# A two-layer decoder trunk on one core: a second half of the input projection resident through a layer, in the room of two of fourteen gather slots

## The reference

```python
def layer(x, ...):
    proj = rmsnorm(x, norm1) @ w_in               # 1024 x 2568: q, k, v, output gate, pooling input, gates
    hm = mlstm_mixer(q, k, v, ...)                # 4 heads of 128, chunks, running-max state
    zp = pool_mixer(u_pool, ...)                  # trailing windows 2, 4, 8, 16
    x = x + concat(hm, zp) @ w_out                # 1024 x 1024
    x = x + peer_ffn(rmsnorm(x, norm2), ...)
    x = x + sigmoid(x @ w_gate) * (p @ w_ple)

def peer_ffn(xn, wq, sub_keys, u_tab, v_tab):
    q = xn @ wq                                   # 1024 x 2048, 8 heads
    # per token and head the best 16 of 128 x 128 product keys
    ue = u_tab[eidx]                              # tokens x 8 heads x 16 experts x 1024
    act = gelu(einsum('td,thkd->thk', xn, ue))
    ve = v_tab[eidx]
    return einsum('thk,thkd->td', gate * act, ve)
```

## Time and profile before

| | |
|---|---|
| runs before | 1910.49 us (1908.98 to 1910.65) |
| the profiled execution, its own time | 1893.48 us |
| its span, first to last instruction | 1891.7 us |
| busy: PE / PE weight load / DVE / ACT / POOL | 1079.0 / 499.7 / 978.1 / 192.3 / 998.2 us |
| mean granted TensorE clock | 0.752 |
| DMA | 685.11 MB, mean 362 GB/s over the span |

### The profile page before, as it was taken

One profiled execution on the slowest core, in us unless ns is written; L12 is line 12 of the kernel. 1 busy time (PEld: TensorE's weight loads), 2 busy tenths in 40 slices (PEclk: granted clock), 3 DMA queues, 4 the chain that ended last, 5 costly groups with the idle time before them and its releaser, 6 DMA issues. The chain is left out here.

```text
span 1891.7 us, 17959 instructions
## 1 busy us (share of the span) xinstructions
PE 1079.0 (57%) x6318; PEld 499.7 (26%) x6318; DVE 978.1 (52%) x2585; ACT 192.3 (10%) x332; POOL 998.2 (53%) x1062
## 2 busy tenths in 40 slices
PE   8840257788955835385655874048885522045556
PEld 4420133433412422241112432024341211031113
DVE  1498975523445788954004576951344497850001
ACT  3200021201101200000000212000110000000002
POOL 0156534345465555656666353755446566656663
PEclk9965668789987967697676886578896765576678
DMA  8699869889999999989999799979999999999995
GB/s 333 244 359 379 337 244 410 337 359 399 357 360 406 423 410 421 404 343 419 371 366 386 256 421 365 408 286 418 368 337 366 402 374 381 396 330 372 368 367 206
DMA packets 172759, 685.11 MB, mean 362 GB/s; under 512 B 19616, under 2 KB 21344, under 8 KB 158190
## 3 DMA queue, kind: packets, MB, share of 16 engines
q0 software_dynamic: 152064, 553.72, 75.9%
q1 hardware_dynamic: 20606, 130.25, 17.3%
HBM read 677.66 MB, written 6.59 MB: 362 GB/s over the span
## 5 line engine op out<-in xcount | busy, mean ns | idle before, releaser
L2105 DVE SCALAR_TENSOR_TENSOR rows<-rows,acc 128x1024 f32<-128x1024 f32 x512 | 594.2, 1217 | 49.6 <-issue 26.7
L908 PE MATMUL bank<-wring,turned 128*128 128x512 f32 (+1 forms) x808 | 394.0, 635 | 40.6 <-DMA wring<-in_w 24.3
L1235 PE MATMUL acc<-rows,wz 128*32 128x512 f32 x1952 | 323.1, 783 | 143.6 <-DMA rows<-in_v,index_tb 102.6
L1450 POOL DMA_INDIRECT rows<-in_u,index_A x256 | 240.3, 939 | 303.2 <-DVE rows L2105 123.8
L1450 POOL DMA_INDIRECT rows<-in_v,index_ta x256 | 242.5, 947 | 234.1 <-PE acc L1235 142.2
L1450 POOL DMA_INDIRECT rows<-in_u,index_B x256 | 240.7, 940 | 179.1 <-DVE rows L2105 110.7
L1450 POOL DMA_INDIRECT rows<-in_v,index_tb x256 | 241.1, 942 | 138.7 <-issue 68.1
L908 PEld LDWEIGHTS bank<-wring,turned 128*128 128x128 f32 x808 | 160.5, 207 | 236.7 <-issue 205.7
L1235 PEld LDWEIGHTS acc<-rows,wz 128*32 128x32 f32 x1952 | 69.6, 130 | 351.9 <-issue 347.0
L1185 PE MATMUL bank<-xn_s,consts 128*128 128x128 f32 x256 | 48.6, 334 | 154.3 <-issue 154.3
L1185 PEld LDWEIGHTS bank<-xn_s,consts 128*128 128x128 f32 x256 | 42.9, 243 | 159.9 <-issue 159.9
(11 more groups left out here) (320 smaller groups left out, 1054.4 us busy)
## 6 DMA issues: line engine op xcount, KB each, us to landing
wring<-in_w SPq DMA_DIRECT2D x103, 1024.0 KB
out_sample<-scratch SPq DMA_DIRECT2D x2, 2128.5 KB
scratch<-in_c_s SPq DMA_DIRECT2D x2, 2064.0 KB
rows<-in_u,index_A POOLq DMA_INDIRECT x256
rows<-in_v,index_ta POOLq DMA_INDIRECT x256
rows<-in_u,index_B POOLq DMA_INDIRECT x256
rows<-in_v,index_tb POOLq DMA_INDIRECT x256
kept<-in_w SPq DMA_DIRECT2D x2, 1024.0 KB
```

The lines of the kernel that those rows point to most:

```text
L908: ins = pe.matmul(ps[:, part], turned["A"][:, 4 * h + c, :], w[:, c, part], start=first, stop=end, skip_group_check=True)
L1235: ins = pe.matmul(acc[i * QUAD:(i + 1) * QUAD, c, :], wz[:, i, at:at + QUAD], row, start=first, stop=end, skip_group_check=True)
L1450: pool.indirect_dma_start(out=rows[:, n % RING, :], out_offset=None, in_=a[table], in_offset=bass.IndirectOffsetOnAxis(ap=which[:, at:at + ...
L2105: dve.scalar_tensor_tensor(u, u, 1.0, acc[:, :, :], ALU.mult, ALU.mult, accum_out=dots[kind][:, s:s + 1]).then_inc(u_used, 1)
```

## The change

`RING` becomes 12, and `kept` holds two halves: those of `project` with row half 0 of column blocks 0 and 1. Each has its own pair of semaphores. SP loads both at the start, and each for layer 1 behind its last use in pass 1. The second half so leaves the ring of three: the list of ring halves goes from 104 to 100, four loads of 1 MB less, and the loads into `kept` go from two to four. 8 KB per partition move from `rows` (two slots of 4 KB) to `kept` (one half of 8 KB). The line numbers behind the first hunk are 1 higher than before, behind the last one 2.

```diff
--- before.py
+++ after.py
@@ -40,11 +40,12 @@
 NEG = -1e30
 REMOVED = -3e38
 
-RING = 14
+RING = 12
 GROUP = 4
 DOTS = 2
 QUAD = 32
 TURN = QUAD // 2
+KEPT = 2
 LANE = 32
 HALF = 2 * P
 LATE = (LANE - DEC) // GROUP
@@ -92,7 +93,7 @@
 
 
 def is_kept(e):
-    return e[0] == "project" and e[2:4] == (0, 0)
+    return e[0] == "project" and e[2] < KEPT and e[3] == 0
 
 
 def half_key(e):
@@ -677,7 +678,7 @@
         sb("to_boundary", P, 96)
         wring = sb("wring", P, WRING, 4, BLOCK)
         rows = sb("rows", P, RING, D)
-        kept = sb("kept", P, 4, BLOCK)
+        kept = sb("kept", P, KEPT, 4, BLOCK)
         keys = sb("keys", P, 2 * PH, NKEYS)
         gain2 = sb("gain2", P, D + HALF)
         x = {"A": sb("x_a", P, D), "B": sb("x_b", P, D), "S": sb("x_s", P, HALF)}
@@ -789,7 +790,7 @@
 
         bank_full = [sem(f"bank_full{i}") for i in range(BANKS)]
         bank_free = [sem(f"bank_free{i}") for i in range(BANKS)]
-        kept_in, kept_used = sem("kept_in"), sem("kept_used")
+        kept_in, kept_used = [sem("kept_in_%d" % j) for j in range(KEPT)], [sem("kept_used_%d" % j) for j in range(KEPT)]
         half_used, u_used, v_used = sem("half_used"), sem("u_used"), sem("v_used")
         wz_clear, xn_ready, squared = sem("wz_clear"), sem("xn_ready"), sem("squared")
         xn_scaled, xn_shown = sem("xn_scaled"), sem("xn_shown")
@@ -862,8 +863,8 @@
             def half(e):
 
                 if is_kept(e):
-                    pe.wait_ge(kept_in, 16 * (layer_of(PASS_TILES[e[1]][0]) + 1))
-                    return kept
+                    pe.wait_ge(kept_in[e[2]], 16 * (layer_of(PASS_TILES[e[1]][0]) + 1))
+                    return kept[:, e[2]]
                 n = HALF_OF[e]
                 if e == APART:
                     pe.wait_ge(last_half_in, 16)
@@ -911,7 +912,7 @@
                     closed(ins, name, t, j)
                 elif is_kept((name, p, j, h)):
                     if t == PASS_TILES[p][-1]:
-                        ins.then_inc(kept_used, 1)
+                        ins.then_inc(kept_used[j], 1)
                 elif t == PASS_TILES[p][-1] and (name, p, j) != ("query", 0, 0):
                     ins.then_inc(half_used, 1)
 
@@ -1336,10 +1337,11 @@
                 sp.dma_start(wring[:, n % WRING].rearrange("p c n -> p (c n)"),
                              a["w"][layer, half_index(e)]).then_inc(half_in[n % WRING], 16)
 
-            def load_kept(layer):
-                sp.dma_start(kept[:, :, :].rearrange("p c n -> p (c n)"), a["w"][layer, IN0]).then_inc(kept_in, 16)
-
-            load_kept(0)
+            def load_kept(layer, j):
+                sp.dma_start(kept[:, j].rearrange("p c n -> p (c n)"), a["w"][layer, IN0 + 2 * j]).then_inc(kept_in[j], 16)
+
+            for j in range(KEPT):
+                load_kept(0, j)
             for e in HALVES_IN_ORDER[0:WRING]:
                 load_half(e)
                 if e == HALVES_IN_ORDER[1]:
@@ -1356,8 +1358,8 @@
                     loaded += 1
                 if is_kept(e) and e[4] == PASS_TILES[1][-1]:
 
-                    sp.wait_ge(kept_used, 2)
-                    load_kept(1)
+                    sp.wait_ge(kept_used[e[2]], 2)
+                    load_kept(1, e[2])
                 if e[0] == "layer":
                     layer = e[1]
                     if layer:
```

## The result

The changed kernel takes 1935.53 us (median of four runs, 1925.05 to 1941.89), the kernel before 1909.74 us beside it. The ratio is 1.0132, 95% interval 1.0081 to 1.0182: slower by some 25 us, four times the forecast and outside the range. Measured twice more it is 1.0143 (1.0097 to 1.0189) and 1.0074 (1.0048 to 1.0101).

What follows compares the result with a forecast made beforehand. The 16 DMA engines were taken as the nearest thing to one bound, with gather, POOL and DVE rates nearly equal. Terms of both signs summed to +6.2 us on 1910.5, said as 1916.5 us; the 8-in-10 range was 1900 to 1932.

Steps and rivals of the forecast that it cites:

- Start: Kernel start: the second kept half loads ahead of `m_s` and the other small loads; +2.4 us.
- Pass 1's wait: Pass 1, at 296.87 us: PE no longer loads the half it waited for; -2 of 2.18 us.
- 519 to 1002 us: DMA-bound stretch: one load saved, shallower ring at handovers, tile 3's front moved among the `vals`; sum +6.5 us.
- Rival D: Much slower: tile 3's front among tile 1's `vals` starves the shorter ring; 1927 to 1932 us, chance 0.12.
- Pass 2's load: In the DMA-bound stretch from 519 to 1002 us: pass 2 no longer loads its half; -2.5 us.
- The stop at 1002 us: Behind `add` of pass 1: four fewer gathers streamed while PE is slow, two more rows behind `embed`; net -2.7 us.
- Start of tile 3's `v`: Two groups ahead of `sample_read` free four slots earlier, -2.5; two fewer slots at the end, +2.5; together 0.
- The stop at 1467 us: Stop from 1467 to 1521 us, built like the one at 1002 us; -2.7 us, bounds -5 to +2.4.
- Start of `v` in pass 3: DMA-bound: two slots +2.5, embedding products before the first group +4.2, products gone from an earlier stop -1; +5.7 us.
- End: Kernel end: one gate product between the last groups instead of two; -1 us.
- Rival B: Faster: ring depth costs nothing, so the slot terms of +2.5 and the +1 are 0; 1905.5 us, chance 0.12.
- The estimate of three gathers in flight: By the skill's DMA rule, an estimated 3.2 us per gather: three in flight would do, further depth only stock against stops.

Runs made afterwards that it cites:

- sets 1 and 4: Two of six measurement sets, on different chips, each with its own runs of the kernel before; the changed kernel's ratio there is 1.0132 and 1.0143.
- sets 1, 3 and 4: Sets whose traces are compared: kernel before traced in 1 and 3 (1893.48, 1905.56 us), changed kernel in 1 and 4 (1941.89, 1935.62 us).
- sets 1 to 5: The first five of six measurement sets; the kernel before takes 1909.7, 1892.8, 1909.7, 1912.2 and 1893.9 us in them.
- the old order: Changed kernel with the work order of the kernel before only around the start of tile 3's `v` rows; 1.0128 of the kernel before.
- old order restored: Changed kernel with the work order of the kernel before from the end of `v` of pass 2 on; 1.0114 of the kernel before.
- the new order alone: Kernel before, with its 14 slots and one kept half, running the changed kernel's order of work; 1.0101, once more 1.0120 of the kernel before.
- depth alone: Kernel before with 12 slots, one kept half and its order of work unchanged; 1.0046, once more 1.0048 of the kernel before.
- set 2: One of six measurement sets, on the same chip as set 3; the kernel before takes 1892.8 us.
- set 6: Last of six measurement sets; the kernel before takes 1732.6 us, the changed kernel 1.0074 of it.
- set 1: First of six measurement sets; the kernel before takes 1909.74 us, the changed kernel 1935.53 us, ratio 1.0132.

## Why the prediction was wrong

The sign was right, the sum was not: +6.2 us against some +26 in sets 1 and 4. By its steps (the traces of sets 1, 3 and 4, two of each kernel, unless others are named):

1. **Start**, +2.4: measured +4 to +5. The wait for `m_s` is the 2.4 us forecast (2.33, and 2.21 in the second trace). What came on top: the first kept half landed later (PE waits 1.95 and 2.97 us for it, before 1.46 and 2.40), and the next products ran at the lower clock.
2. **Pass 1's wait**, -2: the wait is gone in both traces, and nothing of it arrives. From the first to the last `u` row of tile 0 it is 244.3 and 245.2 us, before 243.9 and 245.9.
3. **519 to 1002 us**, +6.5: from the same group of `v` of tile 0 (the 22nd) to the last row of pass 1 it is 500.0 and 499.4 us, before 489.5 and 494.0: +5 to +11, so the sum is right and its terms are not. 5 us are lost before pass 1. The moved front gave 20 us to the `u` rows and took 24 from the `v` rows; I priced only the second, at +2. Rival D named the place and not the gain beside it. "Pass 2's load" was sized at its bytes, 2.5 us; on twelve slots it is worth 10 to 13 us in pass 1, by a path that no trace names.
4. **The stop at 1002 us**, -2.7: the sign and the size hold. From the last row of pass 1 to DVE's first row behind `embed` it is 48.7 and 48.2 us, before 51.8 and 54.2; up to the 49th `u` row it is 1 to 8 us shorter. In sets 1 to 5 this time goes with the number of gathers that stand behind `add`: 51.0 to 52.2 with 28 of them (14 slots and 14 rows, or 12 and 16), 47.8 to 50.5 with 26 (12 and 14, or 10 and 16). POOL's longest wait there is no shorter (24.9 us), against what I gave as a sign.
5. **Start of tile 3's `v`**, 0: measured +10, and the old order takes 8 of it back in that stretch, though the total of that run does not show them. **This is the step that failed.** I took two groups put ahead as four slots freed sooner. They are not freed sooner: `sample_args` had moved too, behind the last `u` row, where it costs 5.5 us and more, and the parts of the order that I had read did not show it. And I did not ask what then stands behind the two groups: `sample_read` left the cover of POOL's wait and came into the stream, and a second wait of 5.4 us appeared.
6. **The stop at 1467 us**, -2.7: the 18.61 us belonged to one execution, and where such a wait comes it outweighs the term. Where it is absent, DVE goes on 32.2 us behind the last `v` row instead of 37.2: one trace of each.
7. **Start of `v` in pass 3**, +5.7: measured +11.6, the largest single loss, and half of it foreseen. The products cost about what I had (old order restored: 36.1 instead of 39.7; but the new order alone, on 14 slots, costs 6.8). The two slots cost 6 to 7.5 us and not 2.5.
8. **End**, -1: measured -0.4 to -3.7 for the last stretch.

Two slots were priced at 2.5 us a handover, one gather after another. The runs with 10, 12, 14 and 16 slots say that this is not a line: nothing from 16 to 14 (with the kept half given up as well), 9 us from 14 to 12, some 34 us from 12 to 10 (across sets). Rival B, that depth costs nothing, is wrong at twelve and, by that one run, right at fourteen. The estimate of three gathers in flight, worked out in the prediction from the Trainium skill, "DMA: Bandwidth & Descriptors", section "Anatomy of one DMA — SWDGE (gpsimd) path", does not size this ring: ten slots are already too few by 2.3%.

So one gain (the wait in pass 1) came to nothing, one handover taken as 0 cost 10 us, and the other had half its price; the terms of steps 3 and 4 hold in their sums. That the parts of step 3 cancelled to the forecast is luck. The range was built from my own bounds, and none of them held a handover at 10 us.

## What to carry to other kernels

When a planner puts a group ahead of other work, read what lands behind it, on every engine: work that stood under a wait costs nothing, and the same work inside the stream costs its length, and more if it then runs slower. In a handover five DVE instructions on one column each cost more here (7.1 us) than the products of a group (1.92). The depth of this ring has a knee between twelve and fourteen slots: each pair below it costs more than the last, and two above it gave nothing. That it lies where the ring just outlasts the longest work between two uses is my reading and not shown. Either way a slot is priced by the handovers and not by the transfer. Before a wait in one trace carries a term, see whether a second execution has it.

## What was not expected of the hardware

In places, with gathers queued, PE goes on at one instruction per 1.4 to 2.8 us though it waits for nothing that the trace shows, here behind `add` of pass 1 (depth alone, set 2):

```profile
1046.40 0.37 PE L912 MATMUL bank<-wring,turned_s 128*32 128x128 f32 x1 [1.09 <-issue]
1049.20 0.37 PE L912 MATMUL bank<-wring,turned_s 128*32 128x128 f32 x1 [2.43 <-issue]
1052.00 0.37 PE L912 MATMUL bank<-wring,turned_s 128*32 128x128 f32 x1 [2.43 <-issue]
```

In set 6 the same products follow each other without a gap, at the same 420 GB/s:

```profile
957.72 1.08 PE L906 MATMUL bank<-wring,turned_s 128*32 128x128 f32 x32
958.74 3.70 PE L909 MATMUL bank<-wring,turned 128*128 128x512 f32 x8
962.37 1.08 PE L906 MATMUL bank<-wring,turned_s 128*32 128x128 f32 x32
```

DVE shows the same: `sample_args` 7.1 us and 0.9 us. In set 6 the kernel before takes 1732.6 us, 9% less than in sets 1 to 5, and the change costs 0.74% and not 1.3 to 1.4. In the changed kernel, the stop behind `add` of pass 1 and its 49 rows take 87.6 us there and 112 in the other sets. So at this place the pace is worth more than all that the change moves there; how much of the 9% it is, the runs do not say. What makes it slow in one set and not in the other no run tells. The loads of instructions that the DMA records show are 51 of 16 KB in the traces of before (set 1), of the changed kernel (set 1) and of set 6, nearly all 0.9 to 1.0 us long, so they do not tell the sets apart. Set 6 was the only one on its chip; but the two sets on one chip differ too, by 0.9% (1892.8 and 1909.7 us), so chip and time of running are not told apart.
